# A two-block transformer on one core: where head spreads and norm sums stand, how squares are added, and products of 258 columns

## The reference

```python
# first block, per layer
x = x + 0.5 * swiglu(rms(x), w_gu, w_down)            # D_FF = 2816
x = x + even_mixer(rms(x)) or odd_mixer(rms(x))       # attention with q and k normalised per head
x = x + memory_cross_attention(rms(x), rms(mem))      # 4 heads of 256, q and k normalised per head
x = x + 0.5 * swiglu(rms(x), ...)
# second block, per layer: as above, with a norm behind each branch
x = x + 0.5 * rms(swiglu(rms(x)))
z = rms(x) @ w_in      # differential attention, an mLSTM in chunks, gates
x = x + rms((g_a * (ya @ w_a) + g_m * (ym @ w_m)) @ w_out)
x = x + 0.5 * rms(swiglu(rms(x)))
def rms(x): return x * rsqrt(mean(x * x) + eps) * gain
```

## Time and profile before

| | us |
|---|---|
| three runs | 2585.99, 2591.59, 2595.99; median 2591.59 |
| the profiled execution | 2594.74 |
| its span, first to last instruction | 2592.9 |
| TensorE busy in the span | 2548.5 (98%), 21,399 instructions |
| VectorE, ScalarE, GpSimd busy | 1801.4, 1388.8, 189.3 |
| mean granted TensorE clock | 0.996 |

### The profile page before, as it was taken

The page is one execution under the profiler, slowest core; times in us unless marked ns, Lnnn a source line. Parts: engine busy times, 40 slices in busy tenths (PEclk is TensorE's granted clock), DMA queues, the critical chain, the costliest instruction groups (busy, mean ns, idle before and its releaser), DMA issues.

```text
span 2592.9 us, 56521 instructions
## 1 busy us (share of the span) xinstructions
PE 2548.5 (98%) x21399; PEld 2478.9 (96%) x21399; DVE 1801.4 (69%) x2897; ACT 1388.8 (54%) x2228; POOL 189.3 (7%) x266
## 2 busy tenths in 40 slices
PE   9999999999999999999999999999999999999998
PEld 8998899999998899999999998999999999989998
DVE  7667586667667585767667758876676686677765
ACT  6456555445445655545445556654454465655543
POOL 0001001000000201000000260000000004300000
PEclk9999999999999999999999999999999999999999
DMA  7654246665554354655654543555555545435553
GB/s 274 209 194 138 91 142 191 228 207 189 192 192 153 101 168 147 195 194 176 208 192 155 186 155 115 170 165 186 185 168 185 183 160 170 142 116 177 179 194 114
DMA packets 123086, 446.41 MB, mean 172 GB/s; under 512 B 13696, under 2 KB 14848, under 8 KB 122944
## 3 DMA queue, kind: packets, MB, share of 16 engines
q1 hardware_dynamic: 120816, 436.79, 51.5%
q0 software_dynamic: 2128, 7.66, 0.9%
HBM read 443.34 MB, written 1.05 MB: 171 GB/s over the span
## 4 chain that ended last, share of the span: by engine, by line
PE 91%; DVE 6%; ACT 1%; issue 1%; DMA 0%; SPq 0%; DVEq 0%; ACTq 0%
PE bank L467 90%; DVE w_lo L1515 1%; PE bank L835 1%; DVE rt L1816 1%; DVE x L1630 1%; DVE z L1626 1%; DVE a L1542 0%; DVE score L1566 0%; DVE rstd_x L1534 0%; DMA x<-in_x_dram 0%; ACT w_hi L1079 0%; DVE z L1752 0%; ACT score L1311 0%; ACT a L1100 0%; DVE z L1842 0%
## 5 line engine op out<-in xcount | busy, mean ns | idle before, releaser
L467 PE MATMUL bank<-a,w_hi 128*128 128x256 f32 x7472 | 1310.3, 279 | 6.4 <-DVE z L1752 4.1
L1515 DVE TENSOR_TENSOR w_lo<-raw,w_hi 128x1024 fp32r<-128x1024 f32 x829 | 1012.5, 1225 | 203.4 <-ACT w_hi L1079 201.7
L467 PEld LDWEIGHTS bank<-a,w_hi 128*128 128x128 f32 x7472 | 1133.5, 188 | 19.7 <-issue 10.9
L467 PE MATMUL bank<-a,w_lo 128*128 128x256 f32 x3736 | 1038.0, 278 | 0.0
L1079 ACT CAST w_hi<-raw 128x1024 fp32r<-128x1024 f32 x829 | 842.7, 1045 | 57.4 <-DMA raw<-in_stream_dram 51.1
L467 PE MATMUL bank<-b,w_hi 128*128 128x256 f32 x4800 | 841.3, 279 | 2.9 <-DVE w_lo L1515 2.9
L467 PEld LDWEIGHTS bank<-b,w_hi 128*128 128x128 f32 x4800 | 727.4, 188 | 9.7 <-issue 4.8
L467 PEld LDWEIGHTS bank<-a,w_lo 128*128 128x128 f32 x3736 | 704.2, 188 | 0.0
L467 PE MATMUL bank<-b,w_lo 128*128 128x256 f32 x2400 | 665.5, 277 | 0.0
L467 PEld LDWEIGHTS bank<-b,w_lo 128*128 128x128 f32 x2400 | 451.4, 188 | 0.0
L1139 ACT CAST b<-hmid 128x256 fp32r<-128x256 f32 x132 | 53.7, 407 | 396.5 <-PE bank L467 385.8
(11 more groups left out here) (200 smaller groups left out, 1904.3 us busy)
## 6 DMA issues: line engine op xcount, KB each, us to landing
raw<-in_stream_dram SPq DMA_DIRECT2D x829, 512.0 KB, 3.5
z<-in_biasc_dram POOLq DMA_DIRECT2D x6, 512.0 KB, 4.7
z<-in_biasa_dram POOLq DMA_DIRECT2D x3, 512.0 KB, 4.8
x<-in_x_dram SPq DMA_DIRECT2D x2, 512.0 KB, 7.8
v<-in_mem_dram POOLq DMA_DIRECT2D x2, 512.0 KB, 7.5
out_dram<-x SPq DMA_DIRECT2D x8, 128.0 KB, 1.8
con<-in_con_dram POOLq DMA_DIRECT2D x1, 784.5 KB, 6.4
heads<-in_heads_dram POOLq DMA_DIRECT2D x1, 512.0 KB, 4.2
```

What stands on the lines that cost most here:

```text
L467: return nc.tensor.matmul(out, lhsT, rhs, start=start, stop=stop, skip_group_check=shared)
L1515: return nc.vector.tensor_tensor(out, a, hi.bitcast(F32), ALU.subtract)
```

## The change

It has five parts.

1. In `sum_squares` VectorE also adds GpSimd's half, and TensorE makes one product instead of two. The sum of `mem` is added by GpSimd alone, seven additions. At the end of a mix stage VectorE adds the squares between the tiles, and TensorE makes two products behind the last tile instead of eight products and one `keep_going`.
2. The wide head sums (`xaq`, `xak`) get their two halves added by GpSimd, and take one product instead of two.
3. In the odd stage and in the mLSTM part of the mix stage the head spreads `hb` come a tile later, and some `hn` and `split` units move with them. `inverse_scale` moves from the `trio` behind the tile `w` 6.
4. In the xa stages one `keep_going` product is added behind the attention.
5. In every third weight tile outside the ffn (`w_next`), and in 12 of the 66 tiles of each ffn, the first of the 24 products is 258 columns wide: it reads the 256 columns of hi and the first two of lo, and writes two columns more in its bank, which nobody reads.

```diff
+BESIDE = 2
@@ before(), odd
-                        hn(*q(1)), w(11), hs(*k(0)), hb("odq", q(0)[1:], q(1)[1:]), w(4), hs(*k(1)), hn(*k(0)), w(5),
-                        hn(*k(1)), w(6), hs(*q(2)), hb("odk", k(0)[1:], k(1)[1:]), w(7), w(12), ("att",), hs(*q(3)), hn(*q(2)), w(13),
-                        hn(*q(3)), w(14), hs(*k(2)), hb("odq", q(2)[1:], q(3)[1:]), w(15), vh(0, 0), hs(*k(3)), hn(*k(2))]
+                        hn(*q(1)), w(11), hs(*k(0)), w(4), hb("odq", q(0)[1:], q(1)[1:]), hs(*k(1)), w(5), hn(*k(0)),
+                        hs(*q(2)), hn(*k(1)), w(6), w(7), hb("odk", k(0)[1:], k(1)[1:]), w(12), ("att",), hs(*q(3)), hn(*q(2)),
+                        w(13), hn(*q(3)), w(14), hs(*k(2)), w(15), hb("odq", q(2)[1:], q(3)[1:]), hs(*k(3)), hn(*k(2)), vh(0, 0)]
@@ between(), odd
-                out[0].append(("hn", "odk", 3, layer, 14, 15))
+                out[0].insert(0, ("hn", "odk", 3, layer, 14, 15))
@@ lstm_between()
-                    2: [spread("diff", 0, 0), w0, diff("hn", 2), w1, diff("hn", 3)],
-                    3: [w0, ("split", 0), ("split", 1), spread("diff", 2, 4), w1],
-                    4: [w0, ("split", 2), ("split", 3), long("hs", 0), w1],
-                    5: [long("hn", 0), w0, long("hs", 1), w1],
+                    2: [w0, spread("diff", 0, 0), w1],
+                    3: [diff("hn", 2), w0, ("split", 0), ("split", 1), diff("hn", 3), w1],
+                    4: [w0, spread("diff", 2, 4), long("hs", 0), w1],
+                    5: [("split", 2), ("split", 3), w0, long("hn", 0), long("hs", 1), w1],
@@ w_tile()
-                    mm(out, wh, hi[:, c, :], c == 0, False)
-                    mm(out, wh, lo[:, c, :], False, False)
-                    last = mm(out, wl, hi[:, c, :], False, c == C - 1)
+                    if beside and c == 0:
+                        mm(out[:, 0:T + beside], wh, both_of[id(hi)][:, c, 0:T + beside], True, False)
+                    else:
+                        mm(out[:, 0:T], wh, hi[:, c, :], c == 0, False)
+                    mm(out[:, 0:T], wh, lo[:, c, :], False, False)
+                    last = mm(out[:, 0:T], wl, hi[:, c, :], False, c == C - 1)
@@ w_next(): every third tile
+                w_tile(at[0], at[0] % RING, out, *act_of[buf], fresh.pop(buf, None), BESIDE * (at[0] % 3 == 0))
@@ ffn on TensorE
-                gate_up(n0 + 4, (s0 + 4) % RING, 2, base + 2)
+                gate_up(n0 + 4, (s0 + 4) % RING, 2, base + 2, BESIDE)
-                        gate_up(n, slot, 4 + u, J)
+                        gate_up(n, slot, 4 + u, J, BESIDE * (1 - u))
@@ head_sums() on TensorE, wide
-                    mm(bank[STAT][:, 0:T], mat, s[:, 0, :], True, False)
-                    last = mm(bank[STAT][:, 0:T], mat, s[:, 1, :], False, True)
+                    last = mm(bank[STAT][:, 0:T], mat, s[:, 0, :], True, True)
@@ attention() on TensorE, xa
+                    if kind == "xa":
+                        keep_going(1)
@@ end of mix on TensorE
                     w_next("b", y_ready)
-                    if k:
-                        sum_chunk(k - 1)
-                keep_going(1)
-                sum_chunk(C - 1)
+                sum_of_all()
                 keep_going(6)
@@ add_squares() on VectorE
+                dve.wait_ge(sq_first, t.next(sq_first))
+                nc.vector.tensor_tensor(sq[:, C // 2, :], sq[:, C // 2, :], sq[:, 0, :], ALU.add).then_inc(sq_second, 1)
@@ end of mix on VectorE
+                    if k == C - 1:
+                        square_added(C - 2).then_inc(sq_second, 1)
+                    if 2 <= k < C - 1:
+                        chain(square_added(k - 1))
@@ GpSimd, units "mem" and "hs"
+                        ins = nc.gpsimd.tensor_tensor(sq[:, 0, :], sq[:, 0, :], sq[:, c, :], ALU.add)
+                        nc.gpsimd.tensor_tensor(s[:, 0, :], s[:, 0, :], s[:, 1, :], ALU.add).then_inc(wide_added, 1)
```

93 lines of the change are left out of this document (55 added, 38 removed).

## The result

The changed kernel takes 2559.9 us (median of 2557.3, 2559.9 and 2574.2), the kernel before 2591.6. The ratio is 0.989, with a 95% interval of 0.985 to 0.993 (it is taken over all runs, so it is not exactly that of the two medians): faster by 1.1%. The profiled execution took 2557.3 us, its span is 2555.4, which is 37.5 us less than that of before. The profiled execution is also the fastest of the three. The prediction was 2548 us, with a range of 2537 to 2574.

What follows compares the result with a forecast made beforehand. TensorE, busy 98% of the span, was taken to bound the kernel: 2594.7 - 16.7 (products) - 10 (waits) - 3.5 (clock) - 17.5 (slow rate) + 0.5 (wide products) = 2547.5, so 2548 us; range 2537 to 2574.

Steps and rivals of the forecast that it cites:

- the first rival: On TensorE's slow rate: the wide products end nothing, 2565 us, or 2557 to 2573 with one ffn different; chance 0.25.
- the stalls come back: Rival: VectorE, with additions between tiles, is late with banks; 8 of 10 us and the clock stay, 2559 us; chance 0.07.
- products removed: TensorE's float32 sum products in `sum_squares`, `mem`, xa and mix: fewer of them, less two added fillers, save 16.7 us.
- waits removed, net: TensorE's waits in the odd, even and mix stages: 11.8 us go, 1.8 come back in new places, so -10 us.
- clock: Odd stage: 7.0 us at half rate follow waits that go, and cost half of themselves, so -3.5 us.
- slow rate ended: FFN 5 and 6, ends of xa and mix stages, mixers: the next wide product ends TensorE's slow rate, -17.5 us.
- wide products: The 167 products with two more columns, in and outside the ffn, cost 0.5 us, from 0.15 to 3.3.
- The cover on VectorE: In `sum_squares`, VectorE's fourth addition of 0.45 us ends 1.2 us before TensorE comes to the sum.
- The cover in cross-attention: In xa the squares end at 326.8 and the sum is made at 330.99; one GpSimd addition takes 0.8, at most 1.3.
- The seven additions for `mem`: On GpSimd from 216.1 on, 0.8 to 0.9 us each, ending at 222 to 222.5, with 0.3 us of new wait.
- The 1.2 us in the even stage: Of TensorE's 2.03 us wait for the spread's multiplications there, 1.2 go because 1.33 us of additions leave VectorE.
- a fast stream that turned slow at a wide product: Sign of the third rival, that wide products break the fast rate in the six fast ffn; chance 0.06, half of it slower.

Runs made afterwards that it cites:

- e10: Changed kernel without wide products and with the old order of head sums and spreads, so mainly the removed products are left; 2579.0 us, 0.993 of the kernel before.
- e4: Changed kernel with two products again in each cross-attention head sum and no GpSimd addition there; 2564.5 us, 0.991 of the kernel before.
- e13: Changed kernel with wide-product pairs only behind interruptions, none in FFN loops, and `rr` made earlier in cross-attention; 2554.1 us, 0.985 of the kernel before.
- e2: Kernel before the change with only the wide products added; 2587.6 us, 0.999 of the kernel before.
- e3: Changed kernel with the old order of head sums, head normalisations and spreads in the odd stage and mixes; 2578.2 us, 0.994 of the kernel before.
- e1: Changed kernel with its 258-column products back at 256 columns, all other edits kept; 2573.3 us, 0.994 of the kernel before.
- e5: Changed kernel with the squares of `mem` added by GpSimd (three) and VectorE (four) instead of GpSimd alone; 2563.5 us, 0.988 of the kernel before.
- e7: Changed kernel with its wide products 272 columns wide instead of 258; 2564.1 us, 0.988 of the kernel before.
- e8: Changed kernel with single wide products behind interruptions and at FFN heads, none in FFN loops, `mem` additions shared with VectorE; 2566.3 us, 0.989 of the kernel before.
- e9: Changed kernel with a second wide product in each tile that has one, 334 in all; 2568.1 us, 0.991 of the kernel before.
- e12: Changed kernel with the start of attention one tile later in both cross-attention stages; 2567.7 us, 0.989 of the kernel before.

## Why the prediction was right, step by step, and where its terms were off

The forecast was faster, 2548 us in a range of 2537 to 2574; measured are 2560. That is inside the range only because the range takes in the first rival: the forecast's own was 2538 to 2558, and 2560 lies just above it, close to the 2559 of the rival "the stalls come back". The direction and the mechanisms hold, most sizes less well, and all that was off but the removed products was off on the same side. The sum went from 2594.7 to 2547.5, 47.2 us; the profiled executions differ by 37.4, and the medians by 31.7.

| term | predicted us | in the traces us | worked out from |
|---|---|---|---|
| products removed | -16.7 | -17.8 | only what is left of 37.5 when the other terms are taken out; by e10 -16.6 |
| waits removed, net | -10 | -4.7 | idle time of TensorE on the page |
| clock | -3.5 | -3.4 | 13.6 to 6.8 us at half rate, half of the difference |
| slow rate ended | -17.5 | -14.9 | 3,366 slow intervals fewer, 4.44 ns each |
| wide products | +0.5 | +3.3 | 167 at 20.0 ns |

**Products removed: right.** e10 measures it with the returned waits in it: 2592.9 less 2578.9 are 14.0 us. Its trace has 2.4 us more of idle time than that of before and 3.4 us more at half rate (1.7), and slow intervals worth 1.5 us fewer: 14.0 + 2.4 + 1.7 - 1.5 = 16.6 us for the 38 products. The cover on VectorE held: no gap ahead of the norm sums for L1561. The cover in cross-attention did not: "one GpSimd addition takes 0.8, at most 1.3" was near (0.92 and 0.97 us at the median, 1.76 at most), no wait for `wide_added` arose, but I looked only at who waits for the addition, not at what TensorE meets when it comes eight products earlier. That is where 2.8 us came back. The fence of rows above shows it; e4 (the wait goes when the products are back) and e13 (it goes when `rr` is early) show that it hangs on both.

**The seven additions for `mem`: mis-sized.** I had them end at 222 to 222.5 (seven of 0.8 to 0.9 from 216.1 on are 221.7 to 222.4) with 0.3 us of wait. They took 7.61 us, the longest 1.8, and end at 223.0:

```profile
215.43 7.61 POOL L2194 TENSOR_TENSOR score<-score 128x256 f32<-128x256 f32 x7 [20.96 <-ACT score L1118]
...
223.19 0.45 PE L471 MATMUL bank<-score,con 128*128 128x256 f32 x1 [1.37 <-POOL score L2194]
```

The shortest, median and longest of the seven are 723, 739 and 1808 ns. The two long ones, 1.6 us from 218.75 on and 1.8 us from 221.24 on, are those beside VectorE's `w_lo`:

```profile
218.16 1.59 DVE L1523 TENSOR_TENSOR w_lo<-raw,w_hi 128x1024 fp32r<-128x1024 f32 x1
...
221.24 1.21 DVE L1523 TENSOR_TENSOR w_lo<-raw,w_hi 128x1024 fp32r<-128x1024 f32 x1
```

The first of these took 1.59 us instead of 1.22; it started while an addition (217.86 to 218.67) was under way, and the next addition, which started 0.59 us behind it, took 1.6 us. By the rule of the Trainium skill (SBUF — State Buffer, "SBUF: two separate sides") the later of the two waits for the other; these rows agree, in both directions. The second pair doesn't settle it: the addition is recorded 9 ns ahead of `w_lo`, and it is the addition that took long. Its price is small here: over the whole execution `w_lo` has a median of 1218 and a longest of 1907 ns, as in the earlier trace rows.

**Waits removed: the failed step.** "Sum 11.8, less 1.8 for waits that come back in new places": gross it was 10.2, and 5.5 came back, not 1.8. All of `recip_two` went, as forecast, and L1842 went from 4.1 to 0.6. In the mLSTM parts two gaps of 1.47 us between a spread and the next tile remain (1576.9 and 2253.5 us), the half that I had left. The 1.2 us in the even stage came to nothing, since the sum of `mem` took its place. The 1.0 us for `pt` in the odd stage did not come: there `pt` rose from 1.6 to 2.4. The rival "the stalls come back" was thus half true, though in other places than it named and without its clock.

**The clock: right in the odd stage**, which is where the prediction had it: 6.8 us at half rate there went. That the whole is -3.4 too is partly luck, since 3.4 us in the second mix went as well and 3.4 came in the even stage. The odd stage holds over many executions. With the old order all four profiled executions (before, e2, e3, e10) have 6.8 or 10.2 us at half rate in the odd stage; with the new one four of ten have 3.4 and six none, and none has one in a mix, where three of the four with the old order do. The even stage has one of 6.8 us near 280 us in every profiled execution but that of before (3.4), whatever the order, and behind the new sum of `mem` a further one of 3.4 in six of ten, which the prediction did not look for.

**Slow rate: right in the mechanism, mis-sized, and not a law.** Of the last three FFN stages, six of nine were slow in the three kernels without wide products (before, e1, e10), two of 33 in the eleven with them. Chance is not excluded for one trace, but for this count it is a poor rival. The 12.6 us that I had for FFN 5 and 6 came true (some 12.4); the 4.9 for the runs at the ends of stages and in the mixers were 2.5. That the slow rate is "a matter of how weight loads and products are aligned" was a guess, and no run tests it: shown is that it lasts and that a wide product can end it. I took the upper end because "little ends the slow rate"; there is a form which neither one, nor two, nor wider products end, and a fresh start behind a float32 product can bring the slow rate back before the next wide one: 2,855 slow intervals are left.

The size over many executions is less settled than the traces make it. Wide products alone bring 0.1% (e2), with the old order and the removed products nothing (e10 0.993, e3 0.994, where the profiled FFN 6 was in the resistant form), with the new order 0.5% (e1 0.994, changed 0.989). The changed kernel has three runs only and its interval touches that of e1, but six further kernels with the new order and wide products (e4, e5, e7, e8, e9, e12) lie at 0.988 to 0.991 too, and four of their intervals end just below where that of e1 begins (0.992). Read the other way, the new order brings 0.5% with the wide products and nothing without them (e10 and e1). The intervals are 0.2 to 0.4% wide on each side, so that one size near 0.25% for each lies just at their edges; why the single traces show more than that of both (12.7 us of slow intervals in e1, 14.6 us of stages in e3) stays open, and so does what each of the two would bring without the other. Shown is which intervals became shorter, not how often an execution has them.

**Wide products: mis-sized.** I took 0.5 of a range of 0.15 to 3.3, "near the lower end". The upper end, from the bumps in the earlier trace rows, is what they cost. By the Trainium skill (TensorE: Matmul & The Clock Gate, "Wait — 56ns, not 53.3ns?") two more columns would add 0.8 ns, an estimate of 0.14 us for 167; the rows have 20.0 ns each. That section has one rate only; the trace doesn't agree.

**Not seen:** a fast stream that turned slow at a wide product. Of the 117 wide products in the fast stretches of the changed kernel none did, nor did any in an FFN of the others.

## What to carry to other kernels

Where an engine is full at a clock of 1.00 and two stretches of one program still differ in count, look at the starts of its instructions: there may be two rates, and which one a stretch has may be settled by how it starts. When work is taken off the bound engine, look up what it meets next at its new, earlier time, since chains of the other engines that were just covered come to light; here a reciprocal of 0.16 us behind one of 1.75. A disturbance that ends a bad rate did so here only in a running stream; right behind an interruption it came too early, and in a fast stream it only cost. And a trace of one execution can show a change at its best: look at several before a term is called measured.

## What the runs showed of the hardware that was not expected

- With 256-column products whose weights change each time, TensorE has stable intervals of 113.3 and 117.8 ns at a granted clock of 1.00. Three products take 340.0 or 353.3 ns.
- One product of 258 columns in a fast stream delays all that follow by 20.0 ns, one of 272 by 33.0. These two, and the 13.3 ns between three slow and three fast products, are within 0.4 ns of multiples of 6.67 ns (3, 5 and 2). What the unit is, no run shows.
- A slow stream has a form that a 258-column product doesn't end (118 122 120 118); it costs some 6.7 ns there and changes nothing (twelve intervals 1420.0 ns for 1413.3).
- Value tiles, in which the activations are loaded and the weights stream, run mostly at the slow spacing in every kernel here (some 940 to 1,180 of their 1,480 intervals).
- GpSimd's addition of 128x256 takes 739 ns at the median and up to 1.8 us beside VectorE's `w_lo`, which took 1.59 for 1.22 where it came second.
